# Local and selected heads in turn, and the compressed branch last, in the prompt attention of a sparse-attention decoder step

## The chip, the cores and the metric

The kernel runs on one core of a Trainium2 chip. The metric is the time of one execution on the device in microseconds; the time before is the median of three runs. A core has five engines that run their own instruction lists in order and meet only at semaphores: TensorE (PE; its weight loads are shown as PEld), VectorE (DVE), ScalarE (ACT), GpSimd (POOL) and SyncE (SP, which here only issues DMAs). Matmuls write to PSUM, of which there are eight banks.

## The reference, cut to what matters

One decoder layer is computed for a prompt of 2048 tokens and for eight sample tokens, in float32. The prompt's attention has 8 heads of 64 channels, two key/value groups of four heads each. Every head has three branches, each with its own softmax, that are added under sigmoid gates:

```python
o_c, p_c = cmp_branch(q, kc, vc, ...)          # against 64 compressed blocks of 32 tokens
idx = select_blocks(p_c, pos)                  # p_c summed over a group's heads -> top 8 of 32 blocks of 64 tokens
o_s = sel_branch(q, ks, vs, pos, idx, rel_bias)  # against the selected blocks only
o_w = win_branch_full(q, kw, vw, rel_bias)     # against the last 512 tokens
o_att = g[0] * o_c + g[1] * o_s + g[2] * o_w
```

So the selected branch of a query needs the compressed probabilities of the same query, of all four heads of a group, first.

## The kernel before, in words

The program runs six stages one after the other: the input projection, the compression of the cache pages, the prompt's keys, the prompt attention, the sample's attention, and the tail (output projection and two gated blocks). Only the prompt attention, `prompt_plan` and `prompt`, is touched.

It works on 16 query tiles q of 128 tokens. A tile has nine items: one `cmp` (all eight heads at once), four `win` (local, five key blocks of 128 at most) and four `sel` (selected, all q+1 key blocks up to the query, those not chosen masked out). Item r of `win` or `sel` is head r of both groups. An item is cut into units of at most four key blocks. `prompt_plan` writes the order of all units out by hand: `turns` is the order in which units are finished, with two more turns a tile, `coef_win` and `coef_sel`, that spread a head's coefficient over its 64 channels by matmuls; `scored[k]` lists the units whose scores are computed at the end of turn k. Scores are computed two items ahead.

What each engine does in a turn:

- TensorE: it transposes the unit's probabilities into one of three banks `ps_p` (L1067; L1062 for `cmp`), multiplies the transposed probabilities of the turn before with the values into an output bank (L1048; L1041 for `cmp`), and computes the scores listed (L1024; L1015 for `cmp`) into one of three banks `ps_s`. Scores of unit n wait until VectorE has emptied half of unit n-1.
- VectorE: `fetch` takes scores from `ps_s`, adds the bias and the mask, and keeps the maximum (L1201 for `win`; L1205 and L1211 for `sel`, the latter for the last two key blocks, whose bias is `mix_bias`); for `cmp` it is L1182 to L1185. Beside that it runs, at fixed turns, `cmp_probs` (L1231 to L1237), `rank` (L1243 to L1247), `choose` (the mask, L1254 and L1256), `coefficients` (L1263, L1265), `cmp_output` (L1272) and `output` (L1278, L1280).
- ScalarE: it copies the transposed probabilities from PSUM (L1120) and takes the exponentials of the next item (L1102, one for each group: the first after the item's first unit, the second after its second unit, or both after the only one), `exp_cmp` (L1107) at the end of local head 0, and the coefficient copy (L1138).
- GpSimd: for each tile it waits for the mask, writes `mix_bias` for eight heads (L1158), and then computes the weight sums of the tail for the tile's share of 40 items (L1147 to L1150): two items in even tiles, three in odd ones.
- SP: for each tile, in this order: it stores the sums of each item of the share and loads the next item (L974, L969), loads the gate rows of tile q+2 (L967), loads the queries of tile q+3 (L962), and waits for the tile's finished output to send it (L995). Each of these waits holds up all that follows in the list.

The outputs of the local heads are summed in bank `O_win`; those of the selected heads and of `cmp` share bank `O_other`. The first value product of an owner waits until VectorE has taken the last owner's result.

In the kernel before the order in a tile is win 0, win 1, cmp of tile q+1, win 2, win 3, sel 0 to sel 3; `choose(q + 1)` is at the end of sel 2, and the first selected head of tile q+1 is fetched at win 2 of tile q+1.

Of the kernel before, what the change touches and what calls it, by code (L numbers as in the profile page):

```python
# [19 lines left out]
ALU = mybir.AluOpType  # L20
# [832 lines left out]
NT = SEQ // 128  # L853
# [5 lines left out]
def prompt_plan():  # L859

    items = [("cmp", 0, 0)]
    for q in range(NT):
        items += [("win", q, 0), ("win", q, 1)] + [("cmp", q + 1, 0)] * (q + 1 < NT) + [("win", q, 2), ("win", q, 3)]
        items += [("sel", q, r) for r in range(4)]
    units, of_item = [], []
    for i, (kind, q, r) in enumerate(items):
        lo = max(0, q - 4) if kind == "win" else 0
        n = 1 if kind == "cmp" else q + 1 - lo
        parts = 1 if kind == "cmp" else -(-n // 4)
        cuts = [lo + n * p // parts for p in range(parts + 1)]  # L870
        of_item.append(list(range(len(units), len(units) + parts)))
        units += [(i, cuts[p], cuts[p + 1] - cuts[p]) for p in range(parts)]

    at = {x: i for i, x in enumerate(items)}
    soft = [i for i, x in enumerate(items) if x[0] != "cmp"]
    rank = {i: n for n, i in enumerate(soft)}
    turns, scored = [], []
    for i, (kind, q, r) in enumerate(items):
        mine = of_item[i]
        ahead = of_item[soft[rank[i] + 2]] if kind != "cmp" and rank[i] + 2 < len(soft) else []  # L880
        for j, u in enumerate(mine):
            turns.append(("unit", u))
            scored.append(ahead[len(ahead) * j // len(mine):len(ahead) * (j + 1) // len(mine)])
        if i == 0:
            scored[-1] = of_item[at["cmp", 1, 0]]
        if kind == "sel" and r == 3 and q + 2 < NT:
            scored[-1] = scored[-1] + of_item[at["cmp", q + 2, 0]]
        extra = []
        if kind == "win" and r == 0 and q:
            extra = [("coef_sel", q - 1)]  # L890
        if kind == "sel" and r == 0:
            extra = [("coef_win", q)]
        if kind == "sel" and r == 3 and q == NT - 1:
            extra = [("coef_sel", q)]
        turns += extra
        scored += [[]] * len(extra)
    first = of_item[0] + of_item[soft[0]] + of_item[soft[1]]
    return items, units, of_item, turns, scored, first


def prompt(nc, d, t):
# [14 lines left out]
    other = [("cmp", 0)] + [x for q in range(NT) for x in [("cmp", q + 1)] * (q + 1 < NT) + [("sel", q)]]  # L916
    other_at = {x: n for n, x in enumerate(other)}
# [5 lines left out]
    with ExitStack() as ctx:  # L923
# [4 lines left out]
        O_win, O_other = pb("ps_ow", [128, 512]), pb("ps_oo", [128, 512])  # L928
# [12 lines left out]
        def upto(eng, s, n):  # L941
            if n > 0:
                eng.wait_ge(s, n)
# [14 lines left out]
        with nc.Block() as block:  # L958
            @block.sync
            def _(sp):  # L960
# [24 lines left out]
                for q in range(NT):  # L985
                    for n in W_SHARE[q]:
                        store_sums(n)
                    if q + 2 < NT:
                        sp.wait_ge(s_oo, other_at["cmp", q] + 1)
                        load_gate(q + 2)  # L990
                    if q + 3 < NT:
                        sp.wait_ge(s_qk, 2 * scoring[last_unit("sel", q, 3)] + 2)
# [10 lines left out]
            def _(pe):  # L1003
# [25 lines left out]
                def values(u):  # L1029
                    i, k0, n = units[u]  # L1030
                    kind, q, r = items[i]
                    pe.wait_ge(s_cp, copies[turn_of["unit", u]] + 2)
                    o = O_win if kind == "win" else O_other
                    if u == of_item[i][0] and r == 0:
                        if kind == "win":
                            upto(pe, s_ow, q)
                        else:
                            upto(pe, s_oo, other_at[kind, q])
                    if kind == "cmp":
                        for g in range(2):  # L1040
                            mm = pe.matmul(o[half(g), :], t["vcp"][:, half(g)], PT[0:64, turn_no[u] % 3, g], start=True, stop=True)  # L1041
# [51 lines left out]
            def _(act):  # L1093
# [16 lines left out]
                for k, (what, x) in enumerate(turns):  # L1110
# [21 lines left out]
                    else:  # L1132
                        b = 0 if what == "coef_win" else 1
                        if b:
                            upto(act, s_oo, other_at["sel", x - 1] + 1 if x else 0)
                        else:
                            upto(act, s_ow, x)
# [26 lines left out]
            def _(dve):  # L1164
# [102 lines left out]
                def cmp_output(q):  # L1267
                    dve.wait_ge(s_pv, turn_no[last_unit("cmp", q, 0)] + 1)
                    dve.wait_ge(s_g[q % 2], 32 * (q // 2 + 1))
                    if q >= 3:  # L1270
                        dve.wait_ge(s_mo[q % 3], 16 * (q // 3))
                    own(dve.tensor_tensor(o(q), O_other[:], t["gate_cmp"][:, q % 2].rearrange("p r n -> p (r n)"), ALU.mult), s_oo, 1)  # L1272

                def output(q, b):
                    kind = "sel" if b else "win"
                    dve.wait_ge(s_pv, turn_no[last_unit(kind, q, 3)] + 1)
                    dve.wait_ge(s_cp, copies[turn_of["coef_" + kind, q]] + 1)
                    own(dve.tensor_tensor(o2[:], (O_other if b else O_win)[:], t["coef_rows"][:, b].rearrange("p r n -> p (r n)"),  # L1278
                                          ALU.mult), s_oo if b else s_ow, 1)
                    ins = dve.tensor_tensor(o(q), o(q), o2[:], ALU.add)  # L1280
                    if b:
# [1 line left out]
                    else:  # L1283
                        step(ins)

                for u in first:
                    fetch(u)
                cmp_probs(0)
                rank(0)
                choose(0)  # L1290
                for k, (what, x) in enumerate(turns):
                    if what != "unit":
                        continue
                    i = units[x][0]
                    kind, q, r = items[i]
                    more = q + 1 < NT
                    for u in scored[k]:
                        fetch(u)
                    if x != of_item[i][-1]:
                        continue  # L1300
                    if kind == "win" and r == 0:
                        if not q:
                            cmp_output(0)
                        if more:
                            cmp_probs(q + 1)
                    if kind == "win" and r == 1 and q:
                        output(q - 1, 1)
                    if kind == "win" and r == 2 and more:
                        rank(q + 1)
                    if kind == "win" and r == 3:  # L1310
                        coefficients(q, 0)
                        if more:
                            cmp_output(q + 1)
                    if kind == "sel" and r == 1:
                        output(q, 0)
                    if kind == "sel" and r == 2 and more:
                        choose(q + 1)
                    if kind == "sel" and r == 3:
                        coefficients(q, 1)
                output(NT - 1, 1)  # L1320


# [899 lines left out]
```

## Time and profile before

| | |
|---|---|
| time, median of 3 runs | 4131.6 us (4129.7 to 4132.03) |
| the profiled execution | 4125.9 us, of which its span 4123.7 us |
| TensorE matmul busy | 3732.4 us, 91% of the span |
| TensorE weight load busy | 3138.0 us, 76% |
| VectorE busy | 1555.3 us, 38% |
| ScalarE busy | 941.6 us, 23% |
| GpSimd busy | 915.1 us, 22% |
| mean granted TensorE clock | 0.952 of full |

The shares are means over stages with different limits. The prompt attention is the stretch from 1056 to 1918 us of the span; what it does is read from that stretch alone.

### The profile page before, as it was taken

The numbers are of one execution on the slowest core, as the hardware profiler recorded it, in microseconds if no ns is written. First come the engines' busy times: TensorE is split into PE (matmuls) and PEld (weight loads), VectorE is DVE, ScalarE is ACT, GpSimd is POOL, SyncE is SP. The second block draws the span as 40 slices with busy tenths as digits, with TensorE's granted clock in tenths as the row PEclk, the third lists the DMA queues.
The fourth block names the chain that finished last, engine by engine and source line by source line (L and its number), as shares of the span: only waits on it lengthen the run. The fifth ranks groups of instructions, "written<-read, shape, count | busy, mean of one in ns | idle before, by whom it ended". The sixth has DMA issues, their size and how long they took to land. (4 is left out here: it accounts for less than half of the span.)

```text
span 4123.7 us, 63576 instructions
## 1 busy us (share of the span) xinstructions
PE 3732.4 (91%) x23087; PEld 3138.0 (76%) x23087; DVE 1555.3 (38%) x3862; ACT 941.6 (23%) x2029; POOL 915.1 (22%) x1145
## 2 busy tenths in 40 slices
PE   7999998655789999995689999999999999999998
PEld 6888886654566777774478888888888888888887
DVE  4344342011666666542042225322253222532223
ACT  1010000000456666663021002210022101221102
POOL 1010101121344322223022123222132221322122
PEclk9999998777699999998699999999999999999999
DMA  4101002986465443314355555555555555555553
GB/s 173 42 16 55 11 29 86 303 249 212 115 173 136 119 116 96 93 45 121 120 169 151 152 152 172 170 151 153 161 168 165 152 153 169 161 144 153 151 151 107
DMA packets 346567, 558.03 MB, mean 135 GB/s; under 512 B 37582, under 2 KB 125006, under 8 KB 345111
## 3 DMA queue, kind: packets, MB, share of 16 engines
q1 hardware_dynamic: 300966, 492.95, 40.2%
q10 hardware_dynamic: 37417, 34.78, 2.8%
q0 software_dynamic: 7904, 26.48, 2.0%
q8 instruction: 188, 3.08, 0.3%
q14 instruction: 92, 0.75, 0.1%
HBM read 480.30 MB, written 78.50 MB: 136 GB/s over the span
## 5 line engine op out<-in xcount | busy, mean ns | idle before, releaser
L319 PE MATMUL ps_z<-x_gained,w_in_sb 128*128 128x257 f32 x2816 | 619.3, 380 | 20.7 <-DVE x_gained L355 20.7
L319 PEld LDWEIGHTS ps_z<-x_gained,w_in_sb 128*128 128x128 f32 x2816 | 532.1, 189 | 102.3 <-issue 21.8
L1120 ACT ACTIVATE PT_pr<-ps_p 128x384 f32<-128x384 f32 (+4 forms) x576 | 256.8, 496 | 247.5 <-PE ps_p L1067 221.2
L1784 PE MATMUL ps_tx<-ff,w_ring 128*128 128x257 f32 x1280 | 305.1, 380 | 7.8 <-DVE ff L1932 7.8
L1784 PE MATMUL ps_ty<-ff_sums,w_ring 128*128 128x257 f32 x1280 | 305.3, 380 | 0.0
L1784 PE MATMUL ps_ty<-h_sums,w_ring 128*128 128x257 f32 x1280 | 304.2, 379 | 0.2 <-issue 0.2
L1784 PE MATMUL ps_tx<-h_gained,w_ring 128*128 128x257 f32 x1280 | 303.3, 379 | 0.0
L1894 POOL TENSOR_TENSOR h<-h,u 128x257 f32<-128x257 f32 x192 | 135.0, 703 | 692.5 <-DVE u L2021 305.3
L1784 PEld LDWEIGHTS ps_tx<-ff,w_ring 128*128 128x128 f32 x1280 | 242.6, 190 | 44.4 <-issue 8.2
L1784 PEld LDWEIGHTS ps_ty<-ff_sums,w_ring 128*128 128x128 f32 x1280 | 243.1, 190 | 36.6
L1784 PEld LDWEIGHTS ps_ty<-h_sums,w_ring 128*128 128x128 f32 x1280 | 242.2, 189 | 36.7 <-issue 0.6
L1784 PEld LDWEIGHTS ps_tx<-h_gained,w_ring 128*128 128x128 f32 x1280 | 241.6, 189 | 35.8
L1815 ACT ACTIVATE ff<-ff 128x257 f32<-128x257 f32 x256 | 107.0, 418 | 703.0 <-DVE ff L1965 703.0
L1102 ACT ACTIVATE S_pr<-S_pr,nmax_pr 128x640 f32<-128x640 f32 (+15 forms) x256 | 251.0, 982 | 29.0 <-DVE nmax_pr L1227 22.9
L1067 PE MATMUL ps_p<-ident,S_pr 128*128 128x128 f32 x1648 | 247.3, 286 | 5.9 <-ACT S_pr L1102 3.9
L1067 PEld LDWEIGHTS ps_p<-ident,S_pr 128*128 128x128 f32 x1648 | 178.8, 143 | 69.8 <-issue 43.9
L575 PE MATMUL ps_cmp<-pages,w_cmp_sb 128*64 128x128 f32 x2048 | 147.4, 317 | 80.2 <-DMA pages<-in_cache_cmp 80.1
L1205 DVE CUSTOM_DVE_ANT_1 S_pr<-ps_s,mask_pr 128x384 f32<-128x384 f32 (+3 forms) x304 | 152.1, 524 | 168.9 <-PE ps_s L1024 168.0
L2000 DVE TENSOR_TENSOR u<-p,ps_ty 128x257 f32<-128x257 f32 x160 | 67.7, 423 | 375.3 <-PE ps_ty L1784 347.2
L575 PEld LDWEIGHTS ps_cmp<-pages,w_cmp_sb 128*64 128x64 f32 x2048 | 143.5, 166 | 84.3 <-DMA pages<-in_cache_cmp 84.0
L1879 POOL TENSOR_TENSOR ff_sums<-ff 128x257 f32<-128x257 f32 x64 | 46.9, 732 | 645.3 <-ACT ff L1815 645.3
L1024 PE MATMUL ps_s<-ks_pr,q_pr 64*128 64x256 f32 (+1 forms) x1232 | 165.0, 385 | 26.4 <-DVE chunk_max_pr L1205 26.3
(293 smaller groups left out, 5466.9 us busy)
## 6 DMA issues: line engine op xcount, KB each, us to landing
w_ring<-scratch_w_sums SPq DMA_DIRECT2D x640, 256.0 KB, 2.6
w_ring<-in_w_tail SPq DMA_DIRECT2D x480, 256.0 KB, 2.6
w_blocks_pr<-in_w_tail SPq DMA_DIRECT2D x40, 1024.0 KB, 8.6
scratch_w_sums<-w_blocks_pr SPq DMA_DIRECT2D x40, 1024.0 KB, 5.3
pages<-in_cache_cmp SPq DMA_DIRECT2D x192, 128.0 KB
pages<-in_cache_cmp ACTq DMA_DIRECT2D x192, 128.0 KB
pages<-in_cache_cmp POOLq DMA_DIRECT2D x128, 128.0 KB, 4.1
w_in_sb<-in_w_in SPq DMA_DIRECT2D x22, 512.0 KB, 13.8
```

What stands on the lines that cost most here:

```text
L319: mm = pe.matmul(o, wg[:, k] if name == "g" else win[:, m, k], aT[:, c % 2, k, h * HF:(h + 1) * HF], start=(k == 0), stop=(k == KT - 1))
L575: mm = pe.matmul(cps[b][64 * g:64 * g + 64, 128 * kv:128 * kv + 128], wc[:, kv, l], pg[b][:, :, g, 64 * kv + 4 * l:64 * kv + 4 * l + 4], s ...
L1024: mm = pe.matmul(sbank(u, g)[:, a:a + w], qt[half(g), r], keys[half(g), 128 * k0 + a:128 * k0 + a + w], start=True, stop=True)
L1067: mm = pe.transpose(tbank(k, g)[:, y], S[:, slot(i), g, base + 128 * y:base + 128 * y + 128], t["ident"][:])
L1102: act.activation(S[:, slot(i), g, 0:n], S[:, slot(i), g, 0:n], ACT.Exp, bias=t["nmax"][:, slot(i), g:g + 1], accum_out=t["rsum"][:, b, 4 * ...
L1120: act.activation(PT[0:rows, turn_no[x] % 3, g, 0:128 * w], tbank(k, g)[0:rows, 0:w], ACT.Copy).then_inc(s_cp, 1)
L1205: ins = dve.tensor_tensor_reduce(blocks(dst(0, near)), blocks(src(0, near)), add, SC, -3e38, ALU.add, ALU.max, cm[:, ncol:ncol + 1])
L1784: mm = pe.matmul(bank[:, 0:HF], w[:, k], b, start=(name in ("P1", "P6", "P5") and k == 0), stop=(name in ("P2", "P4", "P3") and k == 3), s ...
L1815: act.activation(x, x, ACT.Square).then_inc(s_fs, 1)
L1879: own(pool.tensor_tensor(z[:, 0, m], quarter(f, "12", m), quarter(f, "11", m), ALU.subtract), s_tf, 1)
L1894: own(pool.tensor_tensor(x, x, held[q][:, j % 2], ALU.add), s_h, 1)
L2000: own.post(tt(U2[:, p], P1[:, p], bY[p][:, 0:HF], ALU.add), s_u2, 1)
```

## The change

The heads of a tile are put in the order win 0, sel 0, win 1, sel 1, win 2, sel 2, win 3, sel 3, and cmp of tile q+1 comes behind them. Both coefficient turns move into sel 3: `coef_win` behind its first unit, `coef_sel` behind its last. The scores of cmp of tile q+2 are computed at the turn of cmp of tile q+1. The output of `cmp` goes to `O_win`, and the selected heads have their bank alone; the semaphore counts follow. VectorE's steps move: `cmp_output(q)` to the first unit of win 0, the selected output of tile q-1 to the end of win 0 ahead of `cmp_probs(q + 1)`, the local output of tile q to sel 3. `choose(q + 1)` stays at the end of sel 2, and the first selected head of tile q+1 is now fetched at sel 3 of tile q.

```diff
-        items += [("win", q, 0), ("win", q, 1)] + [("cmp", q + 1, 0)] * (q + 1 < NT) + [("win", q, 2), ("win", q, 3)]
-        items += [("sel", q, r) for r in range(4)]
+        for h in range(4):
+            items += [("win", q, h), ("sel", q, h)]
+        items += [("cmp", q + 1, 0)] * (q + 1 < NT)
...
-        if i == 0:
-            scored[-1] = of_item[at["cmp", 1, 0]]
-        if kind == "sel" and r == 3 and q + 2 < NT:
-            scored[-1] = scored[-1] + of_item[at["cmp", q + 2, 0]]
-        extra = []
-        if kind == "win" and r == 0 and q:
-            extra = [("coef_sel", q - 1)]
-        if kind == "sel" and r == 0:
-            extra = [("coef_win", q)]
-        if kind == "sel" and r == 3 and q == NT - 1:
-            extra = [("coef_sel", q)]
-        turns += extra
-        scored += [[]] * len(extra)
+            if kind == "sel" and r == 3 and j == 0:
+                turns.append(("coef_win", q))
+                scored.append([])
+        if kind == "sel" and r == 3:
+            turns.append(("coef_sel", q))
+            scored.append([])
+        if kind == "cmp" and q + 1 < NT:
+            scored[-1] = of_item[at["cmp", q + 1, 0]]
...
                     if q + 2 < NT:
-                        sp.wait_ge(s_oo, other_at["cmp", q] + 1)
+                        sp.wait_ge(s_ow, 2 * q + 1)
                         load_gate(q + 2)
...
-                    o = O_win if kind == "win" else O_other
+                    o = O_sel if kind == "sel" else O_win
                     if u == of_item[i][0] and r == 0:
-                        if kind == "win":
-                            upto(pe, s_ow, q)
+                        if kind == "sel":
+                            upto(pe, s_oo, q)
                         else:
-                            upto(pe, s_oo, other_at[kind, q])
+                            upto(pe, s_ow, 2 * q + (kind == "win"))
...
+                late = of_item[soft_items[1]]
                 for u in first:
+                    if u == late[0]:
+                        cmp_probs(0)
+                        rank(0)
+                        choose(0)
                     fetch(u)
-                cmp_probs(0)
-                rank(0)
-                choose(0)
...
                     if kind == "win" and r == 0:
-                        if not q:
-                            cmp_output(0)
-                        if more:
+                        if j == 0:
+                            cmp_output(q)
+                        if final and q:
+                            output(q - 1, 1)
+                        if final and more:
                             cmp_probs(q + 1)
-                    if kind == "win" and r == 1 and q:
-                        output(q - 1, 1)
-                    if kind == "win" and r == 2 and more:
+                    if kind == "win" and r == 2 and final and more:
                         rank(q + 1)
-                    if kind == "win" and r == 3:
+                    if kind == "win" and r == 3 and final:
                         coefficients(q, 0)
-                        if more:
-                            cmp_output(q + 1)
-                    if kind == "sel" and r == 1:
-                        output(q, 0)
-                    if kind == "sel" and r == 2 and more:
+                    if kind == "sel" and r == 2 and final and more:
                         choose(q + 1)
                     if kind == "sel" and r == 3:
-                        coefficients(q, 1)
+                        if j == 0:
+                            coefficients(q, 1)
+                        if j == min(1, len(of_item[i]) - 1):
+                            output(q, 0)
```

## Rows read from the trace of the kernel before

**Rows 1.** Windows: stretch, length, busy time of each engine, granted clock, DMA.

```profile
1056.00:1918.00 862.00, 783.87 (x7786) 590.04 (x7788) 523.96 (x1962) 528.84 (x1136) 278.32 (x288) 0.96 0.40 113
...
1240.00:1918.00 678.00, 628.22 (x6490) 479.77 (x6488) 398.08 (x1501) 426.05 (x853) 192.93 (x199) 1.00 0.35 99
...
1192.00:1199.00 7.00, 6.52 (x43) 5.12 (x44) 4.11 (x15) 1.57 (x4) 0.00 (x0) 0.55 0.92 288
```

**Rows 2.** Waits of TensorE, 1240 to 1918 us: total us, times, longest.

```profile
PE ps_s L1024 <- DVE chunk_max_pr L1205: 24.4, 24, 3.1
...
PE ps_s L1024 <- DVE chunk_max_pr L1201: 13.3, 18, 2.0
...
PE ps_s L1015 <- DVE chunk_max_pr L1201: 7.4, 10, 0.7
```

**Rows 3.** Order of time on GpSimd: start, us, instruction, idle time before it.

```profile
1132.52 4.62 POOL L1158 TENSOR_TENSOR mix_bias_pr<-band_sb,mask_pr 128x256 f32<-128x256 f32 x8
...
1161.05 5.05 POOL L1158 TENSOR_TENSOR mix_bias_pr<-band_sb,mask_pr 128x256 f32<-128x256 f32 x8
```

**Rows 4.** Order of time on SP: the send of tile 0's output.

```profile
1102.95 0.36 SPq L995 DMA_DIRECT2D scratch_mixT<-o_att_pr  x1
```

**Rows 5.** Order of time on VectorE, tiles 1 and 2.

```profile
1135.46 0.42 DVE L1211 CUSTOM_DVE_ANT_0 S_pr<-ps_s,mix_bias_pr 128x256 f32<-128x256 f32 x1 [1.65 <-POOL mix_bias_pr L1158]
...
1144.77 0.69 DVE L1272 TENSOR_TENSOR o_att_pr<-ps_oo,gate_cmp_pr 128x512 f32<-128x512 f32 x1 [5.19 <-DMA gate_cmp_pr<-scratch_gT]
```

**Rows 6.** Order of time on VectorE, from tile 8 to tile 9.

```profile
1443.46 0.88 DVE L1182 TENSOR_TENSOR S_cmp_pr<-ps_s,cband_pr 128x256 f32<-128x256 f32 x2 [0.69 <-PE ps_s L1015]
...
1446.41 0.20 DVE L1263 RECIPROCAL rec_pr<-rsum_pr 128x8 f32<-128x8 f32 x1
...
1450.34 0.69 DVE L1231 TENSOR_REDUCE csum_pr<-S_cmp_pr 128x8 f32<-128x512 f32 x1
...
1453.02 0.42 DVE L1201 CUSTOM_DVE_ANT_0 S_pr<-ps_s,band_sb 128x256 f32<-128x256 f32 x1
```

**Rows 7.** Groups by line and shape on VectorE, 1240 to 1918: busy, mean ns | idle.

```profile
L1278 DVE TENSOR_TENSOR o_tmp_pr<-ps_ow,coef_rows_pr 128x512 f32<-128x512 f32 x11 | 7.6, 692 | 0.4
...
L1272 DVE TENSOR_TENSOR o_att_pr<-ps_oo,gate_cmp_pr 128x512 f32<-128x512 f32 x10 | 6.9, 692 | 0.3
...
L1184 DVE TENSOR_SCALAR cmax_pr<-cmax_pr 128x8 f32<-128x8 f32 x10 | 5.1, 512 | 0.3
```

**Rows 8.** Order of time on TensorE, tile 9's local heads 0 and 1.

```profile
1451.26 0.70 PE L1024 MATMUL ps_s<-kw_pr,q_pr 64*128 64x256 f32 x4
1451.90 0.88 PE L1067 MATMUL ps_p<-ident,S_pr 128*128 128x128 f32 x6
1452.70 0.66 PE L1048 MATMUL ps_ow<-PT_pr,vw_pr 128*64 128x128 f32 x8
1453.60 0.92 PE L1024 MATMUL ps_s<-kw_pr,q_pr 64*128 64x256 f32 x8 [0.23 <-DVE chunk_max_pr L1201]
...
1456.25 0.66 PE L1067 MATMUL ps_p<-ident,S_pr 128*128 128x128 f32 x4
1456.84 1.07 PE L1041 MATMUL ps_oo<-PT_pr,vcp_sb 64*64 64x512 f32 x4
1457.84 0.92 PE L1024 MATMUL ps_s<-ks_pr,q_pr 64*128 64x256 f32 x8
```

**Rows 9.** Groups by line and shape on ScalarE, 1056 to 1918: a long exponential.

```profile
L1102 ACT ACTIVATE S_pr<-S_pr,nmax_pr 128x1920 f32<-128x1920 f32 x8 | 15.2, 1896 | 1.9 <-DVE nmax_pr L1227 1.9
```

**Rows 10.** Order of time on ScalarE: copies of tiles 1 and 3.

```profile
1110.19 0.66 ACT L1120 ACTIVATE PT_pr<-ps_p 128x256 f32<-128x256 f32 x2 [0.20 <-PE ps_p L1067]
...
1114.22 0.66 ACT L1120 ACTIVATE PT_pr<-ps_p 128x256 f32<-128x256 f32 x2 [0.45 <-PE ps_p L1067]
...
1169.55 1.08 ACT L1120 ACTIVATE PT_pr<-ps_p 128x512 f32<-128x512 f32 x2 [0.67 <-PE ps_p L1067]
...
1172.64 1.08 ACT L1120 ACTIVATE PT_pr<-ps_p 128x512 f32<-128x512 f32 x2 [0.61 <-PE ps_p L1067]
```

More of the change, by code:

```diff
@@ L915, in prompt @@
     turn_no = {x[1]: n for n, x in enumerate(x for x in turns if x[0] == "unit")}
-    other = [("cmp", 0)] + [x for q in range(NT) for x in [("cmp", q + 1)] * (q + 1 < NT) + [("sel", q)]]
-    other_at = {x: n for n, x in enumerate(other)}
     bc = lambda a, n: a.rearrange("p (h o) -> p h o", o=1).to_broadcast([128, a.shape[1], n])
@@ L927, in prompt @@
         tp_ = [pb(f"ps_p{i}", [128, 4, 128]) for i in range(3)]
-        O_win, O_other = pb("ps_ow", [128, 512]), pb("ps_oo", [128, 512])
+        O_win, O_sel = pb("ps_ow", [128, 512]), pb("ps_os", [128, 512])
         S, SB, PT, gn = t["S"], t["S_cmp"], t["PT"], t["gates_tok"]
@@ L1134, in _ @@
                         if b:
-                            upto(act, s_oo, other_at["sel", x - 1] + 1 if x else 0)
+                            upto(act, s_oo, x)
                         else:
-                            upto(act, s_ow, x)
+                            upto(act, s_ow, 2 * x)
                         act.activation(t["coef_rows"][:, b], tbank(k, 0)[:], ACT.Copy).then_inc(s_cp, 1)
@@ L1271, in cmp_output @@
                         dve.wait_ge(s_mo[q % 3], 16 * (q // 3))
-                    own(dve.tensor_tensor(o(q), O_other[:], t["gate_cmp"][:, q % 2].rearrange("p r n -> p (r n)"), ALU.mult), s_oo, 1)
+                    own(dve.tensor_tensor(o(q), O_win[:], t["gate_cmp"][:, q % 2].rearrange("p r n -> p (r n)"), ALU.mult), s_ow, 1)
                 def output(q, b):
@@ L1277, in output @@
                     dve.wait_ge(s_cp, copies[turn_of["coef_" + kind, q]] + 1)
-                    own(dve.tensor_tensor(o2[:], (O_other if b else O_win)[:], t["coef_rows"][:, b].rearrange("p r n -> p (r n)"),
+                    own(dve.tensor_tensor(o2[:], (O_sel if b else O_win)[:], t["coef_rows"][:, b].rearrange("p r n -> p (r n)"),
                                           ALU.mult), s_oo if b else s_ow, 1)
@@ L1296, in _ @@
                     more = q + 1 < NT
+                    j, final = of_item[i].index(x), x == of_item[i][-1]
                     for u in scored[k]:
                         fetch(u)
-                    if x != of_item[i][-1]:
-                        continue
                     if kind == "win" and r == 0:
-                        if not q:
-                            cmp_output(0)
-                        if more:
+                        if j == 0:
[3 more added lines that the diff above has]
+                        if final and more:
                             cmp_probs(q + 1)
-                    if kind == "win" and r == 1 and q:
-                        output(q - 1, 1)
-                    if kind == "win" and r == 2 and more:
+                    if kind == "win" and r == 2 and final and more:
                         rank(q + 1)
-                    if kind == "win" and r == 3:
+                    if kind == "win" and r == 3 and final:
                         coefficients(q, 0)
-                        if more:
-                            cmp_output(q + 1)
-                    if kind == "sel" and r == 1:
-                        output(q, 0)
-                    if kind == "sel" and r == 2 and more:
+                    if kind == "sel" and r == 2 and final and more:
                         choose(q + 1)
                     if kind == "sel" and r == 3:
-                        coefficients(q, 1)
+                        if j == 0:
+                            coefficients(q, 1)
+                        if j == min(1, len(of_item[i]) - 1):
+                            output(q, 0)
                 output(NT - 1, 1)
```

## The prediction

> **What bounds the kernel now.** I began with the page, whose busy shares stand in the table above: TensorE leads. I then cut out the stretch that the change touches, the prompt attention from 1056 to 1918 us, by windows [rows 1]. TensorE is busy for 783.9 of its 862.0 us, VectorE and ScalarE for about 61% each, GpSimd for 32%. So the most that any new order of the same work can give is TensorE's idle time, 78.1 us: 49.8 us in the last eleven tiles (from 1240 on), the other 28.3 us in the first five. Nothing behind 1918 us reads the order of the heads, so the rest of the span is taken as unchanged.
>
> Who ends those idle times in the later tiles stands in the waits [rows 2]: 24.4 + 13.3 + 7.4 = 45.1 of the 49.8 us end with a VectorE instruction that empties a score bank. The reason is in the `scored` lists. While the four short local heads run, the two heads that are scored ahead are in half of the cases long selected heads, so a local turn must score two units where a selected turn scores one, and the second one waits for VectorE.
>
> The early tiles are bound by something else, which the order of time on GpSimd and SP shows [rows 3, 4]. GpSimd adds the mask to the bias (`mix_bias`, L1158) for tile q only after the weight sums of tile q-1's share. In tile 1 the share has three items. Its second item is loaded only when SP has got past the sending of tile 0's output (o_att at 1102.95), and then load and sums follow one another twice, until the mix of tile 2 starts at 1132.52, which is 29.6 us after that send. VectorE, which has chosen the mask long before, waits 1.65 us for the mix, until 1135.46; SP sits in the same chain, and the gate rows that it loads at the end of it cost another 5.19 us [rows 5]. So in the kernel before the chain is just about hidden.
>
> **The change part by part.** All matmuls, copies and exponentials stay; 272 units of local and selected heads, 16 compressed units and 32 coefficient steps change places.
>
> *The scoring.* With local and selected heads in turn, the head scored ahead is always of the running head's kind, so each turn scores one unit. The 45.1 us of score waits lose their cause. What is late next I work out at three places, for the eleven tiles from 5 on.
>
> (a) Compressed output and local heads now share one bank. The first value product of local head 0 waits for `cmp_output`, and behind that product stand TensorE's next scores, for which VectorE waits. After the scores of the next compressed unit, VectorE has: the compressed fetch, 2.95 us (1443.46 to 1446.41), the fetch of a two-block local unit, 0.77 (two halves of 0.42 that overlap a little), and `cmp_output`, 0.69 with 0.03 to the next [rows 6, 7]. That is 4.4 us, or some 4.1 (an estimate) where its small L1184 runs without GpSimd beside it. TensorE meanwhile has two transposed blocks 0.59, the compressed values 1.00 (both read as the distance of starts), scores 0.64 and three transposed blocks 0.80: 3.0 us [rows 8]. The wait is 1.1 to 1.4; I take 1.2, times 11 tiles is 13 us. It is bounded by 0 (VectorE ahead) and by the 3.0 us that TensorE works meanwhile, if it can't start at all.
>
> The small L1184 in the compressed fetch took 0.512 in the mean of the later tiles [rows 7]. The Trainium skill (SBUF — State Buffer, SBUF: two separate sides) says that GpSimd and VectorE, in its two-port modes or with two inputs from that memory, take a shared port pair as an exclusive lock, and the loser waits for a whole instruction. By the rule the compressed fetch would be shorter in its new place, where GpSimd waits for a load, and by the mean row it would not: 12 against 15 us for (a).
>
> (b) At the end of local head 0, VectorE now does the selected output of the tile before and the compressed probabilities one behind the other: fetch of three blocks 1.27 (an estimate: 0.77 and a half more, and the maximum), output 2 x 0.72 [rows 7], probabilities 2.68 (1450.34 to 1453.02), half a fetch and its signal 0.58: 6.0 us. Before, the same chain without the output ended at 1453.60, where TensorE had waited 0.23 us [rows 6, 8]. TensorE can work ahead by two turns less one scoring, 4.06 us with three-block units and 5.05 with four-block ones. Ten tiles give 1.0 to 1.9 us each, 17 us in sum, bounded by the 0.23 seen and by 2.7, if nothing covers the probabilities. Queued behind the late fetch are TensorE's next scores.
>
> (c) ScalarE must now take both exponentials of a selected head within one local head. For 1920 columns one is 1.9 us [rows 9], with some 0.1 to read its sum; with the copies of the local head's five blocks, some 1.3 (two blocks take 0.66 [rows 10]), this is 5.3 us against 4.6 us of TensorE (0.59 + 0.80 transposes, 0.64 + 0.85 scores, 0.59 + 1.1 values [rows 8]). TensorE can begin with the selected head's first half, so I take a wait of 0.2 us from 1400 columns on, growing to 1.0 at 2048, three times a tile, over the last seven tiles some 11 us. Bounds are 0 and, if nothing overlaps, 25.
>
> Together 41 us stand in place of 49.8. Small waits that I can't see in the old rows will be added, so I count a gain of 6 us in the later tiles, with -25 and +10 as its ends.
>
> *The mask chain in the early tiles.* The mask for tile q+1 is still chosen at the end of selected head 2, but it is now wanted one local head later, in the scores issued during selected head 3; before, it was wanted at the next tile's local head 2. VectorE stops in that fetch until the fifth of eight mixes is done (2.9 of 4.62 us [rows 3]). In an odd tile the mix comes 29.6 us after SP's send of the output before, so 32.5 us in all. From that send, which follows local head 0, seven heads remain. In tile 1 a head takes 2.0 us (copies at 1110.19 and 1114.22 are two heads apart [rows 10]), and with the probabilities and the new waits I get 18 us: a stop of 14 us. In tile 3 a head takes 3.1 us (1169.55 to 1172.64), so 25 us: a stop of 8 us. In tile 5 and later, with two units a head, 35 us: none. Even tiles have two items, some 18 us, and stop nothing. During such a stop VectorE holds up the coefficients, with them TensorE and ScalarE, and the tile's output, whose send lets SP go on with the chain.
>
> From the 22 us I take off what the same chain cost before and now doesn't: 1.65, and the gate rows' 5.19 [rows 5], since `cmp_output` comes later. I add 1 us for TensorE's clock: after the lull before 1192 its granted share was 0.55, that is mostly the lower of its two levels (1.2 GHz), and 6.5 us of work there ran at half speed [rows 1]; two longer lulls replace two like it. This makes +16 us, between +4 (the output sent earlier by the tighter order) and +26 (each stop some 2 us longer, and more work at the lower level).
>
> *The rest.* SP's wait before the gate rows is now for `cmp_output` in local head 0, done before SP gets there: 0, hidden by the weight sums; uncovered it would cost the 5.19 us seen. ScalarE's `exp_cmp` comes behind a longer exponential; VectorE gets there only after the output, so 0, at most 1 us a tile. The coefficient matmuls move as they are. The last tile ends with the same output: 0.
>
> **The sum.** +16 - 6 = +10 us on the profiled execution's 4125.9 us (span 4123.7). This run was 5.7 us under the median of 4131.6 us, to which I add: 4141.6, say 4142 us.
>
> **The rivals.** *Balance wins.* The score waits go and VectorE keeps ahead, since it is busy for only 59% of the later tiles (398.1 of 678 us): (c) is nothing and (a) and (b) are 18 us together, a gain of 32 us, and the early stops cost 12. This gives 4112 us. It decides if TensorE's idle time from tile 5 on is under 25 us. For it speaks that nearly all the late waits have one cause; against it, that (b) is seen in the trace already and only gets longer. The Trainium skill (Perfetto Trace Analysis, Optimization Strategy) says that where the most-contended engine changes between regimes, interleaving the regimes may help; by that rule alone the 45 us go, and the time is 4087 us.
>
> *The wait moves to ScalarE.* If the selected head's transposes can't start before both exponentials are done, (c) is 25 us instead of 11, and at the joints of tiles VectorE's queue adds some 5 us: 4161 us. For it: the 5.3 against 4.6 us. Against it: the first half is released by itself.
>
> *A wash.* The stop of tile 3 falls away and with it the lower clock, because tile 2 is long enough for the chain to get ahead, and the late gain stays at 6: 4133 us. For it: the mix of tile 3 was 28.5 us behind that of tile 2 [rows 3], no more than a tile. Against: SP's send holds the chain anew in each odd tile.
>
> **How the numbers follow.** Forecast 0.42, balance 0.22, ScalarE 0.18, wash 0.18. I take 0.2%, 8.3 us, as what can be told from no change. The forecast's own 4132 to 4152 us lies for 0.26 above that bound and for 0.16 below; balance gives 0.21 faster and 0.01 same; ScalarE is slower; wash gives 0.15 same and 0.03 slower. So faster 0.21, same 0.32, slower 0.47. The range from 4116 to 4160 leaves out the deeper half of balance and half of ScalarE.
>
> **What would show it.** In the changed profile: VectorE waiting for the mix (L1158's releaser) twice, some 10 us each, before tiles 2 and 4; TensorE's waits for score banks down from 45 to under 25 us in the later tiles, most of them at local head 0; a wait of about 1 us at the local value products for `cmp_output`; waits of transposes for exponentials growing from tile 9 on. If the mix wait stays under 5 us in sum, the forecast is wrong.

## The result and the profile after

The changed kernel takes 4188.9 us (median of 4 runs, 4185.2 to 4194.9), the kernel before, run beside it, 4131.8 us (4129.7 to 4140.1). The ratio is 1.0134 with an interval of 1.0118 to 1.0149: slower by 57 us, where 10 us were forecast, and outside the range. The profiled execution of the changed kernel took 4185.2 us, of which its span is 4183.3 us.

First the windows (stretch, length, busy us and instructions of PE, PEld, DVE, ACT and POOL, granted clock, DMA share, GB/s). Of the changed kernel: the whole stage, which answers to the first row of [rows 1], its early part, and the later tiles, cut from the first copy of tile 5 to the last copy of the stage:

```profile
1058.00:1978.00 920.00, 802.76 (x7788) 597.27 (x7790) 513.48 (x1966) 536.38 (x1135) 276.12 (x288) 0.93 0.38 106
1058.00:1264.00 206.00, 156.55 (x1304) 109.22 (x1306) 122.27 (x461) 102.71 (x280) 88.44 (x97) 0.79 0.55 153
...
1270.30:1977.20 706.90, 639.11 (x6395) 481.93 (x6395) 386.79 (x1490) 429.67 (x847) 183.24 (x188) 0.98 0.33 93
```

And the later tiles of the kernel before, cut at the same two events:

```profile
1243.50:1916.20 672.70, 623.66 (x6423) 475.67 (x6422) 396.62 (x1496) 424.27 (x848) 189.43 (x193) 1.00 0.35 99
```

The later tiles are longer by 34.2 us: TensorE is idle for 67.8 instead of 49.0 us, and busy with the same matmuls for 15.4 us more, since the granted clock is 0.98 and no longer 1.00. So two things went wrong there, and only one of them is a wait.

Who ends the idle time shows in the waits of the changed kernel (total us, times, longest), 1264 to 1978 us, which answer to [rows 2]:

```profile
PE ps_p L1061 <- ACT S_pr L1096: 32.0, 26, 2.1
PE ps_s L1018 <- DVE chunk_max_pr L1199: 19.8, 12, 2.2
PE ps_ow L1042 <- DVE o_att_pr L1266: 14.5, 11, 2.4
...
ACT S_pr L1096 <- DVE nmax_pr L1221: 30.3, 32, 1.8
```

Of the 45 us of waits for score banks 20.7 are left, as forecast (under 25), and 18.1 of them are (b), scores behind the long VectorE turn at the end of local head 0: one wait in each of tiles 5 to 14. Beside them stand (c), transposes that wait for ScalarE's exponentials, 32 us, and (a), local values that wait for `cmp_output`, 14.5 us.

In the early tiles, VectorE in order of time (start, us, instruction, idle time before it and what ended it) answers to [rows 5]:

```profile
1134.61 0.43 DVE L1205 CUSTOM_DVE_ANT_0 S_pr<-ps_s,mix_bias_pr 128x256 f32<-128x256 f32 x1 [12.06 <-POOL mix_bias_pr L1152]
...
1136.91 0.43 DVE L1205 CUSTOM_DVE_ANT_0 S_pr<-ps_s,mix_bias_pr 128x256 f32<-128x256 f32 x1 [1.65 <-POOL mix_bias_pr L1152]
...
1211.81 0.42 DVE L1205 CUSTOM_DVE_ANT_0 S_pr<-ps_s,mix_bias_pr 128x256 f32<-128x256 f32 x1 [5.29 <-POOL mix_bias_pr L1152]
...
1214.11 0.43 DVE L1205 CUSTOM_DVE_ANT_0 S_pr<-ps_s,mix_bias_pr 128x256 f32<-128x256 f32 x1 [1.65 <-POOL mix_bias_pr L1152]
```

The chain that feeds the first of these stops, on SP and GpSimd (answering to [rows 3, 4]), and its effect on TensorE:

```profile
1105.26 0.37 SPq L989 DMA_DIRECT2D scratch_mixT<-o_att_pr  x1
```

```profile
1128.84 1.26 POOL L1141 TENSOR_TENSOR w_blocks_pr<-w_blocks_pr 128x512 f32<-128x512 f32 x1 [8.74 <-DMA w_blocks_pr<-in_w_tail]
...
1133.96 4.63 POOL L1152 TENSOR_TENSOR mix_bias_pr<-band_sb,mask_pr 128x256 f32<-128x256 f32 x8
```

```profile
1138.19 1.97 PE L1077 MATMUL ps_p<-ident,coef_pr 128*64 128x128 f32 x16 [14.65 <-DVE coef_pr L1259]
```

The mix comes 28.7 us after the send (29.6 us before), GpSimd having waited 8.74 us for a load. After the send it comes no later than it did; it is wanted earlier. The mask itself had been ready since 1120.16.

For this and all later runs I cut the span at the first copy of the stage, tile 5's first copy, and the stage's last copy. Idle is TensorE's; low is the time in that part for which the granted clock was at the lower level. All are us of one profiled execution; "again" is a second profile of the same kernel.

| kernel | start | early | late | late idle | late low | rest |
|---|---|---|---|---|---|---|
| before | 1061.8 | 181.7 | 672.7 | 49.0 | 3.4 | 2207.4 |
| before, again | 1071.2 | 174.4 | 676.9 | 48.8 | 13.7 | 2213.5 |
| after | 1069.0 | 201.3 | 706.9 | 67.8 | 34.1 | 2206.0 |
| after, again | 1064.9 | 199.8 | 709.3 | 69.8 | 34.1 | 2211.8 |
| e2_output_early | 1067.6 | 190.4 | 687.7 | 54.6 | 20.5 | 2211.5 |
| e3_thin_shares | 1066.3 | 175.2 | 705.3 | 69.3 | 27.3 | 2211.7 |
| e4_cmp_later | 1066.6 | 198.6 | 688.7 | 58.1 | 10.2 | 2208.4 |
| e7_exp_in_two | 1067.9 | 205.4 | 680.9 | 48.3 | 23.9 | 2212.7 |
| e6_before_thin | 1064.7 | 168.8 | 683.3 | 52.3 | 20.5 | 2206.4 |
| e10_all_but_exp | 1066.9 | 164.6 | 679.2 | 49.2 | 6.8 | 2212.3 |
| e9_all_moved | 1068.2 | 166.6 | 650.2 | 26.3 | 0.0 | 2208.3 |

In every row late is 621 to 627 us, plus its idle time, plus half of its time at the lower level. So the two columns account for it. Over the two profiles of each, the change costs 22 us early and 33 us late; start and rest agree within 2 us.

### The profile page after: what moved, and what is told of

Same layout as the page of the kernel before. It is cut to its first block and busy times, and to the rows that moved or that the text cites. A ratio compares the mean times of both kernels' runs of the same rounds, so it can differ in the third digit from the quotient of the medians.

```text
span 4183.3 us, 63593 instructions
## 1 busy us (share of the span) xinstructions
PE 3748.2 (90%) x23087; PEld 3142.5 (75%) x23087; DVE 1542.3 (37%) x3862; ACT 950.1 (23%) x2029; POOL 914.5 (22%) x1145
## 5 line engine op out<-in xcount | busy, mean ns | idle before, releaser
L1114 ACT ACTIVATE PT_pr<-ps_p 128x512 f32<-128x512 f32 (+4 forms) x576 | 261.3, 495 | 254.5 <-PE ps_p L1061 238.5
L1061 PE MATMUL ps_p<-ident,S_pr 128*128 128x128 f32 x1648 | 256.5, 290 | 34.9 <-ACT S_pr L1096 33.9
L1873 POOL TENSOR_TENSOR ff_sums<-ff 128x257 f32<-128x257 f32 x64 | 46.9, 733 | 645.1 <-ACT ff L1809 645.1
```

The source lines that it names most:

```text
L1061: mm = pe.transpose(tbank(k, g)[:, y], S[:, slot(i), g, base + 128 * y:base + 128 * y + 128], t["ident"][:])
L1114: act.activation(PT[0:rows, turn_no[x] % 3, g, 0:128 * w], tbank(k, g)[0:rows, 0:w], ACT.Copy).then_inc(s_cp, 1)
L1873: own(pool.tensor_tensor(z[:, 0, m], quarter(f, "12", m), quarter(f, "11", m), ALU.subtract), s_tf, 1)
```

## The experiments

Each ratio is to the kernel before, run beside it on the same chip.

**Both kernels once more.** Nothing is edited.

> The changed kernel once more, with a second profile, to see what of its loss stays from one execution to the next. If the lower granted clock in the later tiles belongs to the new order, the later tiles take 700 us or more again (706.9 in the first profile), with 25 us or more at the lower level; if it comes and goes, the later tiles take 685 to 695 us with the same waits (idle 65 to 70 us) and under 15 us at the lower level. The stage starts 6 to 8 us later than in the kernel before if that offset belongs to the program, and within 2 us of 1061.8 if not.

> The kernel before once more, with a second profile. If its later tiles hold the full clock by their order, they take 670 to 675 us again, with under 8 us at the lower level; if the clock comes and goes, they may take 680 to 690 us with the same 49 us idle. The stage starts within 1 us of 1061.8 us if the offset of 7 us belongs to the program.

Measured: 4187.9 and 4137.9 us, one run each. In the changed kernel the later tiles and their clock repeat: 709.3 us, 34.1 us low. The old order's clock does not quite hold: 13.7 us low. The later start is not the program's, as it came to 1071.2 us with the old kernel. The first matmul on the cache pages shows where that begins, in the old kernel's first and second profile:

```profile
747.45 9.56 PE L575 MATMUL ps_cmp<-pages,w_cmp_sb 128*64 128x128 f32 x128 [9.73 <-DMA pages<-in_cache_cmp]
```

```profile
753.20 4.11 PE L575 MATMUL ps_cmp<-pages,w_cmp_sb 128*64 128x128 f32 x36 [13.95 <-DMA pages<-in_cache_cmp]
```

**e2: the selected output before the fetch of the next turn.**

```diff
+                    if kind == "cmp" and q:
+                        output(q - 1, 1)
...
-                        if final and q:
-                            output(q - 1, 1)
```

> The changed kernel with one step moved: the selected output of the tile before is taken at the turn of the compressed unit, where VectorE waits for scores, and no longer at the end of local head 0. Theory: TensorE's later-tile idle time is a sum of three separate waits, 14.5 us for cmp_output, 18.1 us for scores behind the output and the compressed probabilities, and 30.6 us for exponentials. Then the second falls from 18.1 to about 4, the others stay, SP gets past its send some 6 us earlier in each odd early tile, and VectorE's 22.4 us wait for the mix falls to about 10: in all 20 to 26 us less than the changed kernel, 4163 to 4169 us. Rival: the waits stand for one late VectorE queue and change places; then the score wait falls and another grows by as much, and the time stays within 6 us of the changed kernel's.

Measured: 4154.1 us, 1.0042 (1.0027 to 1.0058). The waits of its later tiles:

```profile
PE ps_p L1061 <- ACT S_pr L1096: 30.7, 28, 2.1
PE ps_ow L1042 <- DVE o_att_pr L1266: 15.8, 11, 2.0
PE ps_s L1018 <- DVE chunk_max_pr L1199: 6.7, 10, 1.1
```

Only (b) falls, by 13 us, so (b) is the output in that turn. The time falls more than expected, since time at the lower level goes with it, 34.1 to 20.5 us. The early mix waits were to fall to about 10 us; they fell only to 18.1 us.

**e3: one item of weight sums in each of the first four tiles.**

```diff
-W_SHARE = [range(len(W_ITEMS) * q // NT, len(W_ITEMS) * (q + 1) // NT) for q in range(NT)]
+W_COUNT = [1, 1, 1, 1, 2, 2, 3, 3, 3, 3, 3, 3, 3, 4, 4, 3]
+W_SHARE = [range(sum(W_COUNT[:q]), sum(W_COUNT[:q + 1])) for q in range(NT)]
```

> The changed kernel with the 40 weight-sum items spread otherwise: one a tile in tiles 0 to 3, two in tiles 4 and 5, three or four later. Theory: the 22.4 us for which VectorE waits for the mix, and about 19 us of lag by tile 4, come from the chain of three items in tiles 1 and 3. Then the mix waits are gone, and the time is 16 to 22 us under the changed kernel's, 4167 to 4173 us. Rival: the early tiles are held by TensorE's lower clock and by their short heads' own latency; the mix wait goes but its time turns into others, and less than 6 us are gained.

Measured: 4160.1 us, 1.0059 (1.0042 to 1.0077), a larger gain than expected. The wait for the mix from 1058 to 1262 us, 22.4 us before the edit:

```profile
DVE S_pr L1207 <- POOL mix_bias_pr L1154: 1.8, 2, 1.1
```

The early part is 26 us shorter and the late part stays: nearly all of the early loss is the mask chain behind the weight sums. Not quite all, since with the same shares the old order's early part is another 6.4 us shorter (175.2 against 168.8 us, e6 in the table).

**e4: compressed scores and probabilities one head later.** Scores at the end of selected head 0, `exp_cmp` and `cmp_probs` at local head 1.

```diff
-        if kind == "cmp" and q + 1 < NT:
-            scored[-1] = of_item[at["cmp", q + 1, 0]]
+        if kind == "sel" and r == 0 and q + 1 < NT:
+            scored[-1] = scored[-1] + of_item[at["cmp", q + 1, 0]]
...
-                        if final and more:
-                            cmp_probs(q + 1)
+                    if kind == "win" and r == 1 and final and more:
+                        cmp_probs(q + 1)
```

> The changed kernel with the scores of the next compressed unit computed at the end of selected head 0 instead of at the turn of the compressed unit, and its exponential and probabilities one local head later. Theory: cmp_output no longer stands behind the compressed fetch, so TensorE's wait of 14.5 us in the later tiles (21.9 us in all) for it goes to near 0, and since the output and the probabilities no longer follow one another, the 18.1 us fall below 5; exponentials stay at 30 us. In all 28 to 38 us less than the changed kernel, 4151 to 4161 us. Rival: VectorE is behind anyway at the head of a tile; the wait moves to the scores of selected head 1 and local head 1, and less than 10 us are gained.

Measured: 4166.5 us, 1.0081 (1.0062 to 1.0101), a miss. The waits of its later tiles:

```profile
PE ps_p L1061 <- ACT S_pr L1096: 23.6, 20, 2.1
PE ps_s L1018 <- DVE chunk_max_pr L1199: 10.0, 10, 1.9
PE ps_ow L1042 <- DVE o_att_pr L1266: 9.9, 11, 0.9
PE ps_s L1009 <- DVE chunk_max_pr L1205: 9.3, 10, 1.0
```

(a) fell only from 14.5 to 9.9 us: `cmp_output` still stands behind the fetch of a local unit, for whose scores VectorE waits. (b) came back in another shape: the compressed scores now wait for a bank at selected head 0 (9.3 us).

**e7: a long selected head's exponential in two pieces**, its first two units within the local head, as before, and the rest at its own first unit.

```diff
+    split = lambda i: items[i][0] == "sel" and len(of_item[i]) > 2
...
+        if j == 0 and split(i):
+            out += [(i, 0, 1), (i, 1, 1)]
...
+                    ends = [0, 128 * sum(units[u][2] for u in us[:2]), 128 * sum(units[u][2] for u in us)]
+                    lo, n = (ends[c], ends[c + 1]) if split(i) else (0, ends[2])
...
+                    if split(i):
+                        step(dve.tensor_tensor(t["rsum"][:, b], t["rsum"][:, b], t["rsum_rest"][:], ALU.add))
```

The selected coefficients move to selected head 3's second unit, since they need the second sum.

> The changed kernel with the exponential of a selected head of three or four units taken in two pieces: the first two units' columns within the local head, the rest at the selected head's own first unit, with a second sum that VectorE adds. Theory: the 30.6 us of TensorE's waits for exponentials in the later tiles come from two long exponentials that must fit into one local head. Then they fall below 5 us at the cost of some 0.3 us of ScalarE for each of 256 more instructions, hidden; 22 to 36 us less than the changed kernel, 4153 to 4167 us, the upper part if the lower clock goes with them. Rival: ScalarE is only the last of several that are late, the selected head's transposes then wait for copies or for banks, and less than 10 us are gained.

Measured: 4165.4 us, 1.0066 (1.0047 to 1.0086). The waits of its later tiles:

```profile
PE ps_s L1037 <- DVE chunk_max_pr L1213: 21.3, 13, 2.2
PE ps_ow L1061 <- DVE o_att_pr L1283: 13.2, 11, 1.5
PE ps_p L1096 <- DVE coef_pr L1276: 7.7, 3, 2.7
PE ps_p L1080 <- ACT S_pr L1117: 4.5, 7, 1.3
```

(c) falls from 32 to 4.5 us, and (a) and (b) stay, so (c) needs the length of the two exponentials that must fit into one local head. The edit adds 64 exponentials, not the 256 instructions of the expectation. The later coefficients give 7.7 us back.

**e6: the thin shares of e3 in the kernel before.**

> The kernel before, its order untouched, with the thin spread of the weight sums (one item a tile in tiles 0 to 3). Theory: in the old order the chain of sums is just hidden, so only the 1.65 us wait for the mix and the 5.19 us wait for gate rows go: 2 to 8 us less than before. Rival: the spread is worth as much here as in the changed kernel, 20 us or more, and then it tells nothing of the new order. Its profile also tells where the prompt attention starts when nothing ahead of it is changed: by the kernel before it was 1061.8 us, by the changed one and its four variants 1066 to 1069.

Measured: 4125.2 us, 0.9980 (0.9971 to 0.9990): some 8 us less, the upper end of what was expected. The early part of this profile, 168.8 us, is under both of the old kernel's. In the changed order the same edit was worth 26 us. So the chain was mostly hidden in the old order, as the prediction had read it, though not wholly: the early part is 6 to 13 us under the old kernel's two. Its later tiles have 20.5 us low with 52.3 us idle, in the old order.

**e10: e2, e3 and e4 together, with `cmp_output` ahead of the fetch.**

```diff
+                    if kind == "win" and r == 0 and j == 0:
+                        cmp_output(q)
                     for u in scored[k]:
                         fetch(u)
```

(The diff shows only what the three others don't; the last two lines are the loop that it stands ahead of.)

> The changed order with the thin spread of the sums, the selected output at the compressed unit's turn, the compressed scores and probabilities later, and cmp_output ahead of the next fetch; exponentials as in the changed kernel. Theory: the later tiles take 622 us of TensorE work at full clock, plus its idle time, plus half the time at the lower clock; of the idle time only the waits for exponentials stay, some 31 us. So the later tiles take 655 to 668 us against 706.9 in the changed kernel and 672.7 before, the early ones 160 to 170 against 201.3 and 181.7: 4100 to 4120 us. Rival: the waits taken away come back as others, and the later tiles stay above 680 us.

Measured: 4125.6 us, 0.9978 (0.9965 to 0.9992), a miss: the later tiles take 679.2 us, 11 us above what was expected and hardly under the rival's 680. (a) is gone (0.4 us) and the early part is 164.6 us, but 19 us of waits for score banks stay, which I had counted as gone, beside 28 us of (c).

**e9: all of it, e10 and e7.**

> The same and the long exponentials in two pieces besides. Theory: the waits for exponentials go too, TensorE has less than 15 us of idle time in the later tiles and hardly any time at the lower clock; they take 630 to 645 us and the early ones 160 to 170: 4076 to 4098 us, under both kernels. Rival: with the other waits gone ScalarE's copies are late, or VectorE is behind by its lumps; the later tiles stay above 660 us.

Measured: 4094.8 us, 0.9909 (0.9892 to 0.9925): faster than both kernels and within what was expected, though the later tiles are not (650.2 us, with 26.3 us idle). Its later tiles, waits and window:

```profile
PE ps_s L1030 <- DVE chunk_max_pr L1221: 9.3, 10, 1.0
PE ps_s L1039 <- DVE chunk_max_pr L1215: 7.9, 11, 1.6
...
PE ps_p L1082 <- ACT S_pr L1119: 2.5, 4, 1.3
```

```profile
1234.80:1884.90 650.10, 623.68 (x6411) 471.90 (x6412) 396.27 (x1499) 440.91 (x976) 214.96 (x212) 1.00 0.42 121
```

TensorE is busy for 623.7 us, as in the kernel before, and idle for 26.3 us instead of 49.0.

## Why the prediction was wrong

**Right: the early tiles.** Forecast were two stops for the mix, 14 and 8 us, and +16 us in all. Measured are 12.06 + 1.65 and 5.29 + 1.65 us, and 19.6 us between the first profiles of the two kernels (25.4 between the second). In the first pair 17.9 of them are idle time of TensorE (43.1 against 25.2 us). In the second 15.0 are, and some 11 are its clock: it worked for 46.9 against 25.5 us at the lower level. So the 1 us that the forecast had for the clock is neither confirmed nor refuted. That a stop lasts until the fifth of the eight mixes, 2.9 us after the first begins, holds too (1133.96 to 1136.91): VectorE goes on after the first of them and stops again.

**Right: the place and nearly the size of (a) and (b).** (a): 13 us forecast, 14.5 measured. (b): 17 us forecast, 18.1 measured at its place, of the 19.8 in its row. TensorE and VectorE at the end of local head 0 of tile 8 show (b) and what it draws after it:

```profile
1428.58 0.88 PE L1042 MATMUL ps_os<-PT_pr,vs_pr 128*64 128x128 f32 x12
1431.63 0.92 PE L1018 MATMUL ps_s<-ks_pr,q_pr 64*128 64x256 f32 x8 [2.18 <-DVE chunk_max_pr L1199]
1432.49 1.03 PE L1061 MATMUL ps_p<-ident,S_pr 128*128 128x128 f32 x6
1433.45 1.55 PE L1042 MATMUL ps_os<-PT_pr,vs_pr 128*64 128x128 f32 x12
...
1437.10 0.88 PE L1042 MATMUL ps_os<-PT_pr,vs_pr 128*64 128x128 f32 x12
```

```profile
1425.53 0.56 DVE L1195 CUSTOM_DVE_ANT_0 S_pr<-ps_s,band_sb 128x384 f32<-128x384 f32 x1 [1.81 <-PE ps_s L1018]
...
1426.80 0.69 DVE L1272 TENSOR_TENSOR o_tmp_pr<-ps_os,coef_rows_pr 128x512 f32<-128x512 f32 x1
...
1428.25 0.69 DVE L1225 TENSOR_REDUCE csum_pr<-S_cmp_pr 128x8 f32<-128x512 f32 x1
...
1430.92 0.56 DVE L1199 CUSTOM_DVE_ANT_1 S_pr<-ps_s,mask_pr 128x384 f32<-128x384 f32 x1
```

From 1425.53 to the end of the half fetch at 1431.48 is the 6.0 us of the sum; TensorE's last work before it ends at 1429.46.

**Wrong: the size of (c), 11 us forecast, 32.0 measured**, beyond its bound of 25. The step that failed is "ScalarE must now take both exponentials of a selected head within one local head ... this is 5.3 us against 4.6 us of TensorE": it let ScalarE begin with the copies of the local head's first unit. One such head in tile 15, on ScalarE, VectorE and TensorE:

```profile
1922.18 0.66 ACT L1114 ACTIVATE PT_pr<-ps_p 128x256 f32<-128x256 f32 x2 [1.81 <-PE ps_p L1061]
1923.72 2.00 ACT L1096 ACTIVATE S_pr<-S_pr,nmax_pr 128x2048 f32<-128x2048 f32 x1 [0.88 <-DVE nmax_pr L1221]
...
1925.72 0.85 ACT L1114 ACTIVATE PT_pr<-ps_p 128x384 f32<-128x384 f32 x2
1926.46 2.00 ACT L1096 ACTIVATE S_pr<-S_pr,nmax_pr 128x2048 f32<-128x2048 f32 x1
```

```profile
1921.81 0.42 DVE L1199 CUSTOM_DVE_ANT_1 S_pr<-ps_s,mask_pr 128x256 f32<-128x256 f32 x1 [1.80 <-PE ps_s L1018]
...
1923.52 0.16 DVE L1221 TENSOR_REDUCE nmax_pr<-chunk_max_pr 128x2 f32<-128x8 f32 x1
```

```profile
1920.64 1.13 PE L1018 MATMUL ps_s<-ks_pr,q_pr 64*128 64x256 f32 x8
...
1926.20 0.66 PE L1061 MATMUL ps_p<-ident,S_pr 128*128 128x128 f32 x4
1928.70 0.63 PE L1061 MATMUL ps_p<-ident,S_pr 128*128 128x128 f32 x4 [1.84 <-ACT S_pr L1096]
```

The head's last scores are issued only in the turn just before (1920.64). VectorE has their fetch and the maximum at 1923.68, and ScalarE, whose copies were done at 1922.84, sits 0.88 us before it can begin. The second group's transposes then wait 1.84 us. This start was missing from the sum: 30.3 us over 32 times, 0.95 each in the mean, and for the 26 waits that is some 25 us, about the 21 that the forecast lacked. The first half was released by itself, as the prediction had it: the rival on ScalarE, at 4161 us the nearest of all, named the engine and had the reason wrong.

In e10 the last tile has heads of both sorts. At its first local head the maximum is there in time and ScalarE begins without a stop; at its second it sits idle for it. On ScalarE and on TensorE:

```profile
1838.37 2.00 ACT L1098 ACTIVATE S_pr<-S_pr,nmax_pr 128x2048 f32<-128x2048 f32 x1
...
1857.10 2.00 ACT L1098 ACTIVATE S_pr<-S_pr,nmax_pr 128x2048 f32<-128x2048 f32 x1 [0.86 <-DVE nmax_pr L1223]
```

```profile
1843.34 0.63 PE L1063 MATMUL ps_p<-ident,S_pr 128*128 128x128 f32 x4 [0.81 <-ACT S_pr L1098]
...
1862.08 0.63 PE L1063 MATMUL ps_p<-ident,S_pr 128*128 128x128 f32 x4 [1.83 <-ACT S_pr L1098]
```

The first wait is near the 1.0 us that the prediction had for 2048 columns, the second is longer by about the late start. The first head also has the compressed values to do, so the two do not differ in the start alone. Nor does a late start by itself cost TensorE much: ScalarE waits 20.5 us for the maximum in the later tiles of the kernel before, where no transposes wait for exponentials, and still 30.3 us in e7, where 4.5 us do. So e7 shows that the length of the pair is needed for (c); that the late start makes up the difference to the forecast is read from the rows, and no run moved it alone.

**Wrong: the clock of the later tiles, not in the sum at all.** The forecast gave 1 us for the clock, in the early tiles only. In the rows above, twelve value matmuls take 1.55 us behind the 2.18 us wait and 0.88 four microseconds later. The windows around them show the granted clock:

```profile
1429.60:1433.00 3.40, 1.36 (x13) 1.27 (x14) 2.74 (x8) 0.44 (x2) 0.00 (x0) 1.00 0.85 279
1433.00:1436.50 3.50, 3.50 (x24) 2.47 (x22) 0.60 (x4) 0.98 (x2) 0.00 (x0) 0.51 0.90 265
1436.50:1440.00 3.50, 3.50 (x38) 2.48 (x36) 2.30 (x14) 2.42 (x6) 1.51 (x2) 1.00 0.27 105
```

The middle one is at 0.51, nearly the lower of the two levels (1.2 GHz), and TensorE is busy for all of it: its matmuls are slow without waiting for anything. Of the nine such stretches in the later tiles, each begins within 2 us of the end of a wait of 1.7 to 2.4 us: four of (b), four of (c) and one of (a). The ten of the second profile lie likewise behind waits of 1.7 to 3.1 us, and so do the old order's nine in its three profiles, behind waits of 1.8 to 3.3 us. What the change adds is such waits: of 1.5 us and more there are 18 and 20 in its later tiles, against 4, 4 and 7 in the old order and 2 in e9, where the clock held. No run changes these waits and nothing else: that they are the cause is argued from the rows, not shown.

In all there are 34.1 us low, and the matmuls take 15.4 us more than in the kernel before. How much of this is the change's stays open: the old order had 3.4, 13.7 and 20.5 us low in its three profiles, the changed one 34.1 twice, so between 7 and 15 us. The prediction's ceiling of 78.1 us for any new order left the clock out too: in the early part of the kernel before TensorE worked for 53.8 us at the lower level, some 27 us more than at the upper one (an estimate, from half the speed).

The later tiles then add up: 32.0 + 19.8 + 14.5 us of waits where 41 were forecast (+25), and 15.4 us of clock, make the 40 us between the forecast's -6 and the measured +34.2.

**The rivals.** The wash and the balance failed by what the forecast named for them: the stops came, and idle time was 67.8 us, over the 25 from which balance decides. Balance is nearly what the order gives once the deadlines are met: e9 is at 26.3 us idle, and 30 us under the old order with the same shares (4094.8 against 4125.2 us, each in ratio to the kernel before 0.9909 and 0.9980). No run gives the old order the other moves of e9; its later tiles have no waits for exponentials that the two pieces could take away. The Trainium skill (Perfetto Trace Analysis, Optimization Strategy) says that interleaving regimes whose most-contended engine differs may improve performance. The interleaved order of e9 is faster; the kernel as it was changed is not.

The compressed fetch did get shorter in its new place: its small L1178 takes 0.238 us in the mean, L1184 before 0.512 [rows 7]. Nine of the ten ran with no GpSimd instruction beside them and took 0.17 us, the tenth, beside one, 0.84. The Trainium skill (SBUF — State Buffer, SBUF: two separate sides) says that of a GpSimd instruction and a VectorE instruction in a two-port mode the one that starts first keeps the shared port pair for its whole length, and the other is blocked. The rows agree with that, though they show neither port nor mode. The (a) of 14.5 us is near the 15 of the mean row all the same: the local output stands right before that fetch, and in tile 8 it puts the fetch off by 0.3 us (compressed scores done at 1419.48, fetch begun at 1419.77).

## What to carry to other kernels

When work of two kinds is interleaved, the mean load of each engine is no longer the question: for each step, write down when its input is issued, and not only how long it and its neighbours take; the start of the first exponential was the term that was missing here. Price the waits that are added by their length as well as by their sum, since waits of about 2 us in a dense stretch were followed by a lower clock, in the changed order about every second time, and it cost up to nearly as much as the extra waits themselves. A reorder that loses may lack only its deadlines: five small moves turned 1.3% slower into 0.9% faster.

## What the runs showed that I had not expected

- TensorE's granted clock fell nine and ten times within the changed kernel's later tiles, in both of its profiles, each time at the end of a wait of 1.7 us or more; in the old order it fell once, three and five times in three executions, behind such waits as well, and in e9 not once.
- The same program started the stage at 1061.8 and at 1071.2 us in two executions, with its first cache page 5.8 us later. An offset between two single profiles ahead of the changed code is no evidence of an effect.
- An edit of the shares worth 26 us in one order was worth 6 to 13 us early, and 0.2% in the whole, in the other: what a hidden chain costs depends on when its result is wanted.
